# Second layer: reciprocal roots as one power on Pool, in place of a root on ACT and a reciprocal on DVE

## The reference, cut to what matters

```python
def rms_norm(x, g):
    xf = x.astype(jnp.float32)
    y = xf * lax.rsqrt(jnp.mean(xf * xf, axis=-1, keepdims=True) + EPS)
    return (y * g.astype(jnp.float32)).astype(x.dtype)
...
def mixer_b(h, w_in, q_gain, k_gain, w_out):
    proj = h @ w_in                                # 512 x 10240: q, k, v of 3 groups x 8 heads, and z
    ...
    for g, (window, dilation) in enumerate(B_PATTERNS):
        q = apply_partial_rotary(rms_norm(qkv[:, :, 0, g], q_gain[g]), cos, sin)
        k = apply_partial_rotary(rms_norm(qkv[:, :, 1, g], k_gain[g]), cos, sin)
        o, lse = dilated_window_attention(q, k, qkv[:, :, 2, g], window // dilation, dilation)
    ...
```

## Time and profile before

| what | us |
|---|---|
| median of 3 runs (lowest, highest) | 3438.44 (3437.16, 3441.84) |
| the profiled execution's own time | 3443.41 |
| its span, first to last instruction | 3441.3 |
| PE busy | 3227.9 (94%) |
| DVE busy | 1839.7 (53%) |
| POOL busy | 1286.7 (37%) |
| ACT busy | 1081.2 (31%) |

### The profile page before, as it was taken

How to read it: one execution, slowest core, us unless ns; L and a number is a source line. 1 busy time by engine, 2 the same in 40 slices (tenths; PEclk the granted TensorE clock), 3 DMA queues, 4 the chain that set the end, 5 groups by cost and what they waited for, 6 DMA issues and landing times.

```text
span 3441.3 us, 38555 instructions
## 1 busy us (share of the span) xinstructions
PE 3227.9 (94%) x16146; PEld 2654.4 (77%) x16146; DVE 1839.7 (53%) x2217; ACT 1081.2 (31%) x1423; POOL 1286.7 (37%) x394
## 2 busy tenths in 40 slices
PE   6999999999999899999999799989999999789998
PEld 5888878787878788779887677756888777568886
DVE  5663567676666363544536566665322475852224
ACT  3222233333333332332222434444222332142222
POOL 3333345242424244434343311125444454444443
PEclk8999999999999999999999899989999999899998
DMA  4443422121212123335544111112333242023331
GB/s 138 141 153 131 162 98 74 49 82 42 86 45 79 62 86 98 95 109 177 171 138 153 61 38 38 38 37 68 116 98 98 86 147 98 13 61 98 98 98 61
DMA packets 278701, 319.99 MB, mean 93 GB/s; under 512 B 6770, under 2 KB 244993, under 8 KB 278338
## 3 DMA queue, kind: packets, MB, share of 16 engines
q1 hardware_dynamic: 239808, 245.38, 22.2%
q10 hardware_dynamic: 38722, 72.15, 6.1%
HBM read 311.22 MB, written 6.29 MB: 92 GB/s over the span
## 4 chain that ended last, share of the span: by engine, by line
PE 75%; DVE 17%; ACT 3%; issue 3%; POOL 1%; DMA 1%; ACTq 0%; DVEq 0%; SPq 0%; POOLq 0%
PE ps L498 21%; PE ps L500 21%; PE ps L499 21%; DVE rs L1906 3%; PE psx L929 2%; PE psx L706 1%; DVE macc L1822 1%; PE ps L961 1%; PE ps L733 1%; PE psx L498 1%; PE psx L499 1%; PE psx L500 1%; DVE KB L1911 1%; PE psx L634 1%; DVE QB L1911 1%
## 5 line engine op out<-in xcount | busy, mean ns | idle before, releaser
L317 POOL TENSOR_TENSOR Wl<-Wr,Wh 128x2048 fp32r<-128x2048 f32 x232 | 1073.5, 4630 | 1745.4 <-ACT Wh L1172 1745.4
L498 PE MATMUL ps<-Ah,Wh 128*128 128x512 f32 x2016 | 812.2, 403 | 28.5 <-DVE Al L1727 15.1
L500 PE MATMUL ps<-Ah,Wl 128*128 128x512 f32 x2016 | 790.3, 392 | 0.0
L499 PE MATMUL ps<-Al,Wh 128*128 128x512 f32 x2016 | 790.2, 392 | 0.0
L1172 ACT ACTIVATE Wh<-Wr 128x2048 fp32r<-128x2048 f32 x232 | 443.1, 1910 | 364.1 <-DMA Wr<-in_w_mlp_in_dram 109.8
L498 PEld LDWEIGHTS ps<-Ah,Wh 128*128 128x128 f32 x2016 | 382.0, 189 | 123.2 <-issue 38.9
L499 PEld LDWEIGHTS ps<-Al,Wh 128*128 128x128 f32 x2016 | 381.8, 189 | 86.3 <-issue 9.4
L500 PEld LDWEIGHTS ps<-Ah,Wl 128*128 128x128 f32 x2016 | 381.3, 189 | 81.4
L498 PE MATMUL ps<-Yh,Wh 128*128 128x512 f32 x1088 | 426.1, 392 | 1.1 <-DVE Yl L1778 1.1
L499 PE MATMUL ps<-Yl,Wh 128*128 128x512 f32 x1088 | 424.1, 390 | 0.0
L500 PE MATMUL ps<-Yh,Wl 128*128 128x512 f32 x1088 | 423.9, 390 | 0.0
(11 more groups left out here) (352 smaller groups left out, 4058.2 us busy)
## 6 DMA issues: line engine op xcount, KB each, us to landing
Wr<-in_a_w_in_dram SPq DMA_DIRECT2D x48, 1024.0 KB, 6.4
modw<-in_w_mod_dram ACTq DMA_DIRECT2D x96, 512.0 KB, 5.5
Wr<-in_b_w_in_dram SPq DMA_DIRECT2D x40, 1024.0 KB, 5.0
Wr<-in_w_mlp_in_dram SPq DMA_DIRECT2D x32, 1024.0 KB, 5.7
Wr<-in_w_mlp_out_dram SPq DMA_DIRECT2D x32, 1024.0 KB, 5.2
Wr<-in_a_w_out_dram SPq DMA_DIRECT2D x16, 1024.0 KB, 5.3
Wr<-in_c_w_in_dram SPq DMA_DIRECT2D x16, 1024.0 KB, 5.7
Wr<-in_attn_w_qkv_dram SPq DMA_DIRECT2D x12, 1024.0 KB, 5.1
```

Source lines behind the costliest of these rows:

```text
L317: pool.tensor_tensor(E.Wl[:, s, :], E.Wr[:, s, :], E.Wh[:, s, :].bitcast(F32), ALU.subtract).then_inc(*LO.did(p))
L498: pe.matmul(o, ah, bh, start=first, stop=False)
L499: pe.matmul(o, ah, bl, start=False, stop=False)
L500: return pe.matmul(o, al, bh, start=False, stop=last)
```

## The change

ACT no longer takes the root: it writes mean square plus epsilon to `rs` (Identity, with the same bias and scale). Pool, ahead of its add of each tile, raises `rs` to the power -0.5 in place; the exponent comes from a second column of `eps`, broadcast over 128x512. DVE's reciprocal and its wait on itself go, and DVE waits for Pool's power in its place. `eps` gets its second value in the preamble, by a second memset.

```diff
@@ pool_program, rope(i, t)
         spare = E.acc[0:32, :] if t % 2 else tmp[0:32, 3, :]
+        pool.wait_ge(*A.of("B", "sqrt", i, t))
+        r = E.rs[:, t % 2, :]
+        pool.tensor_tensor(r, r, E.eps[:, 1:2].to_broadcast([P, S]), ALU.pow).then_inc(*G.did("B", "rinv", i, t))
         pool.wait_ge(*V.of("B", "rp", i, t))
         pool.tensor_tensor(q, q, spare, ALU.add).then_inc(*G.did("B", "rope", i, t))
@@ act_program, sqrt(i, t)
-            act.activation(rs[:, r, :], psx[:, 2 + r, :], ACT.Sqrt, bias=eps[:, 0:1], scale=1.0 / P).then_inc(*A.did("B", "sqrt", i, t))
+            act.activation(rs[:, r, :], psx[:, 2 + r, :], ACT.Identity, bias=eps[:, 0:1], scale=1.0 / P).then_inc(*A.did("B", "sqrt", i, t))
@@ dve_program, preamble()
-        dve.memset(eps[:], EPS).then_inc(*V.did("eps"))
+        dve.memset(eps[:, 0:1], EPS).then_inc(*V.did())
+        dve.memset(eps[:, 1:2], -0.5).then_inc(*V.did("eps"))
@@ dve_program, rest(i, t)
             dve.wait_ge(*A.of("B", "sqrt", i, t))
-            dve.reciprocal(rs[:, r, :], rs[:, r, :]).then_inc(*V.did())
-            dve.wait_ge(*V.now())
+            dve.wait_ge(*G.of("B", "rinv", i, t))
             dve.wait_ge(*A.of("B", "cp", i, t))
```

## The result

The changed kernel takes 7340.14 us (median of 4 runs, 7339.52 to 7342.47) against 3440.14 us before on the same chip: 2.134 times as long, 95% interval 2.130 to 2.138. That is +3900 us where +401 was forecast, far outside the range of 3460 to 4300. The sign was right and the size was not.

The account below looks back on a forecast made before the run. PE bounds the kernel, DVE pacing the query and key tiles. With 9 us a power, 48 x 9 - 39 for Pool's loop + 8 for the clock = +401 us on the 3438.4 median: 3839 us, range 3460 to 4300.

Parts of the forecast that it names:

- The price of the power: Duration x of one power on Pool over 128x512, estimated at 9 us from DVE's division factor.
- far dearer: Rival: Pool's power takes over 18.6 us, done element by element in software; at 30 us, 4847 us; chance 0.12.
- 48x - 39: Time added over four passes by Pool's loop, in us, with x the duration of one power.
- 80.5 + 12x: Pool's time per pass, first split's end to twelfth add's end: 12 powers at 4.42 us extra, six splits.
- The loop and its pair, 2x + 13.42: Pool's chain of power, DVE's part and add: x + 4.42 us a tile, 2x + 13.42 a pair with split.
- The cost of ACT's part: ACT's 48 roots become affine copies in the same place over the same 128x512; costed at nothing.
- L1911 always at 0.75 us: DVE's product never meets a Pool split in the new order, so 0.75 us, never 3.15.
- POOL's busy time up by 48x: Sign of being right: Pool's busy time rises by the 48 powers, each of duration x.
- The gain that the stage could give: PE's waits for splits and value copies in the query and key tiles: 15.6 us, 0.45%, at most.
- The clock: PE's lower granted clock after waits, counted in each pass's last value tiles: 2 us a pass, 8 us together.
- L317: Sign of being right: PE's waits for this line in the second layer grow to some 400 us.
- PE waits for ACT: Sign of being wrong: PE waits for ACT or a transfer instead of at L317; no size given.

Follow-up runs that it names:

- experiment 1: Changed kernel with a plain product in place of Pool's power, reciprocal root left out: 3454.19 us against 3442.08 for the kernel before, ratio 1.0039.
- experiment 5: Changed kernel with powers over 128x64 and other exponents, bases and a full-tile exponent by tile: 3912.37 us, measured once.
- plain: The same run as experiment 1: changed kernel with a plain product in place of the power, 3454.19 us.
- cols64: Changed kernel with the power over the first 64 of 512 columns alone: 3917.36 us, ratio 1.1386 to the kernel before.
- shapes: Changed kernel with the power over six shapes by tile, from 128x1 to 32x512: 5873.43 us against 3442.08 for the kernel before, measured once.
- experiment 6: Changed kernel with ACT taking the root again and Pool raising it to -1: 7341.56 us, measured once.
- experiment 8: Kernel before without the reciprocal, the root used in its place, nothing changed on Pool: 3423.01 us against 3440.75, ratio 0.9942.
- experiment 3: The same run as cols64: changed kernel with the power over 64 of 512 columns, 3917.36 us.
- experiment 7: Changed kernel with the next tile's full power put ahead of the wait for the add in Pool's queue: 7221.68 us, measured once.

## Why the prediction was wrong

**The step that failed is "The price of the power".** It says "I take 9 us, between one and two, as an estimate; the bounds are 0.55 below, 1.27 as the lowest likely value, and 18.6 above". The power takes 81.92 us. The step carried over to Pool the factor that a division costs on DVE, 4.9 plain passes. On Pool a power costs 81.92 / 1.03 = some 80 plain products (the changed kernel and experiment 1). DVE's factor did not carry over, and no row of the kernel before had any function on Pool at all. What the routine does in those 159 ns a column stays open. 18.6 was thus no bound but a third guess in the same unit, and the range closed on it. With no row to show a price, the top should have stayed open, or the rival "far dearer" should have had far more than its 0.12; even that rival named 30 us. The Trainium skill's figure (GPSIMD Engine Reference, section 3.1) for a branch on data, 5.1 us by my estimate, was still further off; experiment 5 shows no cost that depends on the data.

**With x measured, the rest of the sum holds:**

| run | x, us | 48x - 39 | with 8 for the clock | measured |
|---|---|---|---|---|
| plain | 1.03 | +10.4 | - | +12.1 |
| cols64 | 10.53 | +466.4 | +474.4 | +475.3 |
| shapes, one run | 0.55 to 81.92, together 2465.1 | +2426.1 | +2434.1 | +2431.4 |
| the change | 81.92 | +3893.2 | +3901.2 | +3900.0 |

The stretch that the sum goes by holds too: in the changed kernel Pool takes 1062.2 to 1062.6 us in each pass from the end of the first split to the end of the twelfth add, and 80.5 + 12x is 1063.5.

So the whole miss of 3499 us is (81.92 - 9) x 48 = 3500.

**Point by point.** The loop and its pair, 2x + 13.42: right, 15.5 us in experiment 1; taking the wait out of it gave -35 us there (3454.19 to 3419.06) and -118.5 us at full price. The cost of ACT's part, nothing: right (experiment 6). L1911 always at 0.75 us: right. POOL's busy time up by 48x: right, 5212.4 - 1286.7 = 3926 us, less what the adds and splits gained. The gain that the stage could give, 15.6 us at the most: too small, 17.7 by the runs and 21.3 by the profiles (experiment 8). The clock, 2 us a pass: near. PE begins again after its longest wait:

```profile
1546.40 0.56 PE L501 MATMUL ps<-Wh,Ah 128*128 128x256 f32 x1 [163.21 <-DVE VB L1949]
```

The two stretches behind it (length, PE busy, granted clock, DMA):

```profile
1546.40:1550.59 4.19, 4.19 (x19) 0.50 0.00 0
1550.59:1560.92 10.33, 9.46 (x79) 0.99 0.00 0
```

Up to 1550.59 the clock is at the lower of its two levels, 1.2 GHz, and the products stand 0.21 us apart; from there on they stand 0.12 apart. From the first of them to the first score it is 14.5, 15.0, 15.1 and 15.3 us in the four passes (1546.40 to 1560.92 in the first), where it was 12.6 before (576.56 to 589.18; the prediction's 11.7 is only the products themselves). That is 9.5 us in all where 8 was put.

Wrong was where PE would be seen to wait. I named L317, "some 400 us", and 409 us stand there, but that is luck, since the forecast was for a power of 9 us. With one of 10.53 us (experiment 3) only 124.8 us stand at L317, beside 170.3 behind ACT's square and 78.7 for the value copies. The first wait that PE meets is now another. In the changed kernel PE waits 2735 us for its sums, behind ACT's square, behind ACT's wait for the `rs` buffer. I had even listed "PE waits for ACT" as a sign of being wrong. It wasn't one: Pool is never idle before a power, so none of these waits is in the loop.

## What to carry to other kernels

Before an operation moves to an engine that the trace has never seen do it, time that one operation: here its price was all of the error, and the time built on top of it held to some us. Ask for room in the queue and not in the busy time: Pool was idle for 63% of the span, and even a product of 1.03 us in the wrong place made the kernel 0.4% slower, while the same product ahead of the wait made it 0.6% faster. And find what the stage can give back (here 0.5%, by leaving the operation out) before choosing where the work goes; ACT had the room for it.

## What the hardware showed that I had not expected

- Pool's power costs 159 ns for each column, for 1 partition as for 128: 0.55 us for 128x1, 81.92 for 128x512. All 128 rows of `rs` hold the same numbers here, so a layout with positions on partitions would need far fewer columns; that wasn't tried.
- The price did not move with the data that were tried: exponents -0.5, 0.3, 1 and 2 and a base of 1 cost the same over 128x64, and -1 the same as -0.5 over 128x512.
- A product on Pool with a broadcast second operand takes 1.03 us over 128x512, where adding two full tiles takes 1.27. Whether the broadcast or the operation makes the difference wasn't separated.
- A power of 82 us slows DVE's product to 1.36 to 1.47 us in place of 0.75 and doesn't hold it until it ends. Beside a split the product ends only behind the split: 3.15 us in the earlier trace rows, 6.15 in experiment 7.
- With PE busy for 16% of a pass the granted clock over the whole pass was 0.57 of full speed, and PE's busy time rose from 3228 to 3342 us for the same matmuls. Some 9.5 us of these 114 reached the end.
